# From the eleventh batch of the first mixer on, TensorE lays the banded mask into the score banks

## The reference, cut to what matters

```python
valid = ((kpos[:, None, :] >= 0) & (kpos[:, None, :] < n)
         & (jnp.abs(qpos[:, :, None] - kpos[:, None, :]) <= A_WINDOW))
...
s_w = jnp.einsum('bqhgd,bkhd->bhgqk', qi, ki).astype(jnp.float32) * scale
s_w = jnp.where(mi[None, None, None], s_w, NEG_INF)
s_c = jnp.einsum('bqhgd,bkhd->bhgqk', qi, kc).astype(jnp.float32) * scale
s_s = jnp.broadcast_to(sink_f, s_w.shape[:-1] + (1,))
p = jax.nn.softmax(jnp.concatenate([s_w, s_c, s_s], axis=-1), axis=-1).astype(v.dtype)
```

## Time and profile before

| what | value |
|---|---|
| median of 3 runs | 2929.58 us (2929.5 to 2929.69) |
| profiled execution, its own time | 2931.75 us |
| its span in the profile | 2929.9 us |
| TensorE busy | 2895.2 us, 99% |
| VectorE busy | 2275.1 us, 78% |
| ScalarE busy | 1253.5 us, 43% |
| GpSimd busy | 167.0 us, 6% |
| batches of mixer A | about 350 to 435 us from the span's start |

### The profile page before, as it was taken

The page is one execution under the profiler, slowest core; times in us unless marked ns, Lnnn a source line. Parts: engine busy times, 40 slices in busy tenths (PEclk is TensorE's granted clock), DMA queues, the critical chain, the costliest instruction groups (busy, mean ns, idle before and its releaser), DMA issues.

```text
span 2929.9 us, 44432 instructions
## 1 busy us (share of the span) xinstructions
PE 2895.2 (99%) x17597; PEld 2808.3 (96%) x17597; DVE 2275.1 (78%) x3460; ACT 1253.5 (43%) x2009; POOL 167.0 (6%) x171
## 2 busy tenths in 40 slices
PE   8999999999999999999999999999999999999999
PEld 6999979999999988999999997899999999989999
DVE  6889887888788877888888877778888887777653
ACT  3332474443333266443333248644333334664432
POOL 0000220000000031000000012000000001320000
PEclk9999999999999999999999999999999999999999
DMA  7655314555555512555555531255555555324342
GB/s 286 210 211 214 150 34 172 184 211 195 186 184 201 213 59 88 194 187 205 188 194 191 206 120 46 73 201 193 198 191 194 193 200 203 109 75 173 128 144 93
DMA packets 87723, 490.22 MB, mean 167 GB/s; under 512 B 11825, under 2 KB 13169, under 8 KB 51377
## 3 DMA queue, kind: packets, MB, share of 16 engines
q1 hardware_dynamic: 83696, 480.42, 44.7%
q0 software_dynamic: 3904, 8.24, 1.1%
HBM read 485.33 MB, written 3.29 MB: 167 GB/s over the span
## 4 chain that ended last, share of the span: by engine, by line
PE 55%; issue 38%; DVE 4%; ACT 2%; DMA 1%; POOL 1%; SPq 0%; DVEq 0%; POOLq 0%; ACTq 0%
PE ps L858 16%; PE ps L877 8%; PE ps L863 8%; PE ps L910 5%; PE ps L1091 4%; PE ps L881 4%; PE ps L842 1%; PE ps L1026 1%; PE ps L1066 1%; PE ps L1173 1%; DMA boot<-in_mod_w 1%; PE ps L1007 1%; PE ps L1011 1%; PE ps L976 0%; PE ps L1109 0%
## 5 line engine op out<-in xcount | busy, mean ns | idle before, releaser
L858 PE MATMUL ps<-h_hi,w_hi 128*128 128x386 f32 x2688 | 908.2, 338 | 0.0
L858 PE MATMUL ps<-h_lo,w_hi 128*128 128x386 f32 x2688 | 893.3, 332 | 0.0
L1651 DVE TENSOR_TENSOR w_lo<-w_raw,w_hi 128x2048 fp32r<-128x2048 f32 (+3 forms) x281 | 703.2, 2502 | 30.1 <-ACT w_hi L1301 29.6
L1678 DVE CUSTOM_DVE_ANT_0 F_junk<-F_slab,cond,mod_b 128x1024 f32<-128x1024 f32 x544 | 706.9, 1299 | 13.1 <-DVE mod L1678 0.5
L1301 ACT ACTIVATE w_hi<-w_raw 128x2048 fp32r<-128x2048 f32 (+3 forms) x274 | 568.3, 2074 | 15.4 <-DMA w_raw<-in_ffn_dn 11.5
L858 PEld LDWEIGHTS ps<-h_lo,w_hi 128*128 128x128 f32 x2688 | 512.5, 191 | 0.0
L858 PEld LDWEIGHTS ps<-h_hi,w_hi 128*128 128x128 f32 x2688 | 503.1, 187 | 0.4 <-ACT w_hi L1301 0.4
L863 PE MATMUL ps<-h_hi,w_lo 128*128 128x386 f32 x2688 | 494.3, 335 | 0.0
L877 PE MATMUL ps<-F_act_hi,w_hi 128*128 128x384 f32 x1408 | 473.6, 336 | 0.0
L877 PE MATMUL ps<-F_act_lo,w_hi 128*128 128x384 f32 x1408 | 473.3, 336 | 0.0
L863 PEld LDWEIGHTS ps<-h_hi,w_lo 128*128 128x128 f32 x2688 | 468.9, 187 | 0.0
(11 more groups left out here) (391 smaller groups left out, 3485.5 us busy)
## 6 DMA issues: line engine op xcount, KB each, us to landing
w_raw<-in_ffn_gu SPq DMA_DIRECT2D x176, 1024.0 KB, 4.8
F_slab<-in_mod_w SPq DMA_DIRECT2D x272, 512.0 KB, 5.6
w_raw<-in_ffn_dn SPq DMA_DIRECT2D x64, 1408.0 KB, 6.5
w_raw<-in_d_w SPq DMA_DIRECT2D x8, 1536.0 KB, 6.7
boot<-in_mod_w SPq DMA_DIRECT2D x8, 1024.0 KB, 10.2
w_raw<-in_a_w SPq DMA_DIRECT2D x4, 1536.0 KB, 6.5
w_raw<-in_b_w SPq DMA_DIRECT2D x4, 1536.0 KB, 6.4
w_raw<-in_c_w SPq DMA_DIRECT2D x8, 544.0 KB, 3.7
```

What stands on the lines that cost most here:

```text
L858: pe.matmul(ps[:, 2 * par + u, 0:N_MOVE], w[0][:, k, u, :], h[:, k, :], start=(k == 0 and h is h_hi), stop=False)
L1651: dve.tensor_tensor(w_lo[par][:, 0:w], w_raw[par][:, 0:w], w_hi[par][:, 0:w], ALU.subtract).then_inc(w_split_lo.sem, 1)
L1678: dve.tensor_tensor_reduce(out=junk[:], in0=w, in1=cond[:, c, :], scale=scale, scalar=mod_b[:, n:n + 1], op0=ALU.mult, op1=ALU.add, accum_ ...
```

## The change

For batches b = 10 to 15 VectorE's addition at line 1987 is dropped. In its place `scores(b)` begins with two matmuls, one for each head's bank, of an identity with a 128x256 mask (zeros on the own block, the triangle on the other). The score products then add to what stands in the bank. GpSimd prepares the three operands once, in the free `h_room`: five instructions on 128x128 between the context gain and the wait for `qn_ready` of group 3. TensorE waits for all five in `scores(10)`.

```diff
+MASK_ON_PE = 10
...
+                        v["mask_wide"] = h_room[0][:, 0:2 * N_LAT].rearrange("p (x c) -> p x c", x=2)
+                        v["ident_r"] = h_room[1][:, 0:P]
...
                         pool.tensor_tensor(v["nrm"][:, 0, :], v["raw"][g % 4][:, 0, 0:heads + HD], v["g"][:],
                                            ALU.mult).then_inc(ctx_ready.sem, 1)
+                        if kind == "A" and g == GROUPS[kind] - 1:
+                            pool.wait_ge(raw_ready.sem, raw_ready.after((s, g), TT - 1))
+                            pool.tensor_copy(v["ident_r"], ident[:]).then_inc(mask_made, 1)
+                            for x in range(2):
+                                pool.tensor_copy(v["mask_wide"][:, x, (1 - x) * P:(2 - x) * P], v["mask"][:, x, :]).then_inc(mask_made, 1)
+                                pool.tensor_scalar(v["mask_wide"][:, x, x * P:(1 + x) * P], v["mask"][:, x, :], 0.0, None,
+                                                   ALU.mult).then_inc(mask_made, 1)
                         pool.wait_ge(qn_ready.sem, qn_ready.after((s, g)))
...
+                masked = kind == "A" and b >= MASK_ON_PE
+                if masked:
+                    if b == MASK_ON_PE:
+                        pe.wait_ge(mask_made, 5)
+                    for i in range(2):
+                        pe.matmul(to(i, at, N_LAT), v["ident_r"][:], v["mask_wide"][:, x, :], start=True, stop=False)
                 if x == 0:
                     for i in range(2):
-                        pe.matmul(to(i, 0, P), query(i, 0), key(i)[:, 0:P], start=True, stop=True)
+                        pe.matmul(to(i, 0, P), query(i, 0), key(i)[:, 0:P], start=not masked, stop=not masked)
...
-                        pe.matmul(to(i, at, N_LAT), query(i, lat), key(i)[:, P:P + N_LAT], start=True, stop=True)
+                        pe.matmul(to(i, at, N_LAT), query(i, lat), key(i)[:, P:P + N_LAT], start=not masked, stop=not masked)
...
-                        mm = pe.matmul(to(i, at + N_LAT, N_PAST), query(i, lat), cache, start=True, stop=True)
+                        mm = pe.matmul(to(i, at + N_LAT, N_PAST), query(i, lat), cache, start=not masked, stop=True)
...
-                if kind == "A":
+                if kind == "A" and b < MASK_ON_PE:
                     blk = both[:, :, at + (1 - x) * P:at + (2 - x) * P]
                     chain.link(dve.tensor_tensor(blk, blk, v["mask"][:, x, :].unsqueeze(1).to_broadcast([P, 2, P]),
                                                  ALU.add))
```

More of the change, by code:

```diff
@@ L373, in build @@
         kv_out = sem("kv_out")
+        mask_made = sem("mask_made")
         pe_step, act_step, dve_step, pool_step = (sem(n) for n in ("pe_step", "act_step", "dve_step", "pool_step"))
```

## The result

The changed kernel took 2936.63 us in the median of 11 runs (2935.8 to 2938.13), the kernel before 2929.89 us beside it (11 runs, 2929.5 to 2932.08). The ratio is 1.0022, with a 95% interval of 1.0014 to 1.0029: 6.7 us slower, between 4.1 and 8.5. The profiled execution took 2937.68 us, with a span of 2935.8 where 2929.9 was before. The forecast of 2933.5 us had the direction and the place, and it was 3.1 us short, 0.3 of them because the kernel before was itself 0.3 us slower in these runs than in the three that the forecast went by. The time lies 0.8 us outside its range.

A forecast was written before the change was run, and what follows sets the result against it. It took the start of batch 14's transposes on TensorE as the stage's bound. A delay of 2.6 us at full clock plus 1.3 for the lower clock gave 3.9 us slower, 2933.5 us, range 2930.9 to 2935.8.

The forecast's parts named there:

- the wait for GpSimd: In round 10 TensorE stands from 405.10 until GpSimd's five instructions (0.37 each, 1.85) end at 409.2, about 4.1 us.
- the low clock: From 409 on TensorE runs at 1.2 GHz for some 3 us, adding 1.3 us (bounds 0 and 1.7).
- the mask pair: Two one-pass TensorE matmuls of 256 columns: 0.3 us, counted in rounds 10, 11, 12, 14, hidden in 13 and 15.
- last output product to the first mask matmul: TensorE ahead of the masks of batch 10, including its stand for GpSimd's preparations: 4.49 us.
- packed stretch at full clock: TensorE from 409.2 to the transposes of batch 9 at 415.97: 6.17 us plus two mask pairs 0.6.
- transposes of 9 to maxima of 12: From 415.97 to about 420.8: the earlier 4.49 us to the end of batch 12's scores, plus one pair, 0.3.
- maxima of 12 to maxima of 14: 7.59 us against 7.75 before: one VectorE mask (0.46) goes, one TensorE pair (0.3) comes.
- maxima of 14 to transposes of 14: From 428.4 to 434.95, with the mask addition of batch 15, about 0.4 us, gone from it.
- What bounds the stage: In mixer A the start of batch 14's transposes, 432.39 before, counts; all that follows moves with it one for one.
- That the clock holds: Rival: TensorE waits for GpSimd but stays at full clock, 2.6 us slower, 2932.2 us; chance 0.15.
- That the additions are saved: Rival: the wait is absorbed and VectorE's removed additions gain 0 to 2.8 us, 2926.8 to 2929.6 us; chance 0.07.
- The one on the other side: Rival: GpSimd's five are slow, 0.9 each giving 6.5 us slower, 2936.1; over 0.2% from 0.76 each; chance 0.13.

The follow-up runs named there:

- The reordered run: Changed kernel with GpSimd's five preparations in another order, the two multiplications first, then the three copies: 2936.87 us, ratio 1.0023.
- the run with the lowest median: Changed kernel with preparation one group earlier, mask pairs only in batches 8, 9, 10, 11, 15, four `hold_clock` products instead of seven: 2928.62 us, 0.9995.

## Why the prediction was wrong in size, step by step

The path was right: the wait, the packed stretch behind it, the lower clock, and one shift of all that follows. Two terms of the sum failed by their size. One is the wait for GpSimd (4.49 us forecast from the last output product to the first mask matmul, 5.72 measured), in which the 0.37 us for each instruction was to cover VectorE's work beside it and covered only the undisturbed price. The other is the low clock (1.3 forecast, 2.26 measured). The price of the mask pair is a third, smaller one.

Forecast and measurement over D, all from the traces above. The clock's share is the packed stretch of 9.12 us less the 6.86 us that it took at full clock.

| step | forecast | measured | more |
|---|---|---|---|
| last output product to the first mask matmul | 4.49 | 5.72 | 1.23 |
| packed stretch at full clock | 6.77 | 6.86 | 0.09 |
| transposes of 9 to maxima of 12 | 4.84 | 4.91 | 0.07 |
| maxima of 12 to maxima of 14 | 7.59 | 7.86 | 0.27 |
| maxima of 14 to transposes of 14 | 6.56 | 6.64 | 0.08 |
| the low clock | 1.3 | 2.26 | 0.96 |

The steps over forecast add up to 2.7 us, and 3.9 + 2.7 is the measured 6.6.

- **What bounds the stage.** Right. The single number, the start of the transposes of batch 14, moved by 6.57 over D, and the medians by 6.7. Behind it the traces run parallel.
- **The wait for GpSimd.** Right in place and in what it turns into: a packed stretch with `hold_clock` in it and no idle at its end. Mis-sized: "I take 0.37 each, 1.85". Undisturbed the five are 3 x 0.28 + 0.54 + 0.52 = 1.90. So the 1.85 met the undisturbed price, but by luck: it was meant to be more than that, under 0.3 each from the copy of 192 columns and the rest for the work beside it. The first two were held by VectorE's lines 1929 and 1931, each with both inputs in SBUF, and took 0.88 and 0.91: the last ended 3.0 us after the first began. Both of VectorE's rows stand in the trace of before too, at 406.53 and 408.06, beside the very place where the five were to go. I had put the spread of line 719 down to "work beside it" and hadn't looked which work, and when. The reordered run shows that the place sets the price, and line 719 shows whose work it is. Its slowest instruction in mixer A, 1.77 us instead of 1.02, began while VectorE's line 1651 was running, again with both inputs in SBUF, and ended 0.88 us behind it (373.79 against 372.91):

```profile
369.55 3.36 DVE L1651 TENSOR_TENSOR w_lo<-w_raw,w_hi 128x3072 fp32r<-128x3072 f32 x1
...
372.02 2.75 POOL L719 TENSOR_TENSOR A_rope<-A_raw,A_sg 128x320 f32<-128x320 f32 x2 [4.42 <-ACT A_raw L1392]
```

In group 3 it is 0.88 again (398.97 against 398.09). So the copy, the multiplication and the product all end their own undisturbed time less 0.12 to 0.14 us behind VectorE's instruction: 0.15 and 0.16 for 0.28, 0.40 and 0.39 for 0.53, 0.88 for 1.02. Line 719's two rows were there before the change was run. The Trainium skill has the rule, in "SBUF — State Buffer", section "Who interferes with whom": a VectorE instruction with two SBUF inputs and a GpSimd instruction that reads SBUF exclude each other for the whole instruction. The trace agrees: the first copy ended at 407.65, 0.15 us behind VectorE's first, the second at 408.52, 0.16 behind its second.

- **The mask pair.** Mis-sized: "0.3 for a pair". It is 0.43 (409.92 to 410.61 at low clock is 0.69; 416.09 to 416.52 at full clock 0.43). That makes it as dear as the addition of 0.46 which it replaces, so the period of the maxima didn't fall to 7.59 us, as I had it, but went up from 7.75 to 7.86. The pair accounts for 7.72 of that (7.75 - 0.46 + 0.43). The rest is that TensorE turns the next keys (line 987) 2.01 us behind the transposes of batch 11, where it was 1.83; why was not tested. The same period is 7.87 in the run with early preparation. The estimate of 0.2 us that was worked out from the Trainium skill ("TensorE: Matmul & The Clock Gate", "Back-to-back issue gap") was further off still.
- **The clock.** Right that it falls, and with TensorE kept busy it stayed up. Mis-sized: "from these shares it was at 1.2 GHz for about 3.4 us" was one stretch, behind 2.07 us idle, and I made its length the upper bound. Here it lasted 6.8 us, 5.0 of them on work. The miss in GpSimd's wait is the larger, but the upper end had room for it, 1.7 us more. For the clock it had 0.4 more, and 0.96 came; for the matmuls 0.2, and the other steps of the table add up to 0.51. These two put the time outside the range, the clock above all.
- **The rivals.** That the clock holds is out. That the additions are saved is out for this kernel; without the wait it is what happens, with 0.4 to 0.9 us (masks from batch 12, early preparation). The one on the other side, at 0.13, named what held GpSimd ("slow beside VectorE's two-input ones") and ended nearest, but not by that alone: GpSimd needed 0.6 each, under its 0.76, and the clock brought the rest. 6.7 us is just over the 5.9 that a measurement tells from no change, with an interval on both sides of it.

What stays open is why the low clock lasted 3.4 us in one place and 6.8 in six others. The one place differs from the six both in the idle time and in the work that followed, and no run separates these. The runs show that its beginning isn't tied to when TensorE resumes: it began 1.84 us ahead of that in the changed kernel and 0.18 ahead in the one that waited for three.

## What to carry to other kernels

An engine at 6% of the span is still late if its new work stands behind a late instruction and a busy engine waits for it at once: write down the time at which the operands can first be ready and the time at which the first reader stands there, and prepare a constant a stage sooner. Price a small GpSimd instruction twice, alone and beside each two-input instruction that VectorE runs at that moment. And when a change makes TensorE idle for longer than any stretch that the trace shows to be harmless (1.66 us here), cost the clock over the work that follows, not over the idle time, and look for products on a constant in that stretch that have lost their reason.

## What the runs showed of the hardware

- GpSimd, 128x128 into the rounded type: a copy took 0.28 us alone and 0.88 to 0.91 beside a two-input instruction of VectorE; a multiplication by a constant 0.52 to 0.54 alone and 0.87 to 1.10 so held. VectorE pays as well: its product of line 1912 took 0.81 us in group 1 of the kernel before, with no GpSimd instruction beside it (the context gain had ended at 359.01), and 1.49 us in group 3, where it begins 0.42 us after GpSimd's context gain and ends 0.68 us behind it. VectorE's timeline of the kernel before:

```profile
359.75 0.81 DVE L1912 TENSOR_TENSOR A_nrm<-A_raw,A_cg 128x640 f32<-128x640 f32 x1
...
406.53 1.49 DVE L1912 TENSOR_TENSOR A_nrm<-A_raw,A_cg 128x640 f32<-128x640 f32 x1
```

- TensorE's clock fell to 1.2 GHz for 6.8 us in every run in which it had stood idle for 3.02, 4.63, 5.06, 5.37 or 5.38 us, and stayed there through several microseconds in which the engine was busy 1.00. Idle stretches of 1.24, 1.39 and 1.66 us did nothing to it, and 2.07 us cost 3.4 us at 1.2 GHz. On this work (a mask pair, scores, three output products, transposes), 5.0 us at the lower clock cost 2.3 us.
- A one-pass matmul pair of 256 columns between products with another stationary operand cost 0.43 us, 0.21 each. In round 8 of the run with the lowest median it stands directly behind the one-pass products of the projection and cost 0.23 (from the last of them to the scores 0.50, and 0.27 without a pair). A plain F32 pair of 128 columns ahead of the products with the cached keys cost 0.84 us.
